# Order of ScalarE's bank copies, and a fifth slot for cached values, in a one-core decoder step

## The chip, the cores and the metric

The kernel runs on one core of one Trainium2 chip. A core has five engines that run their own instruction streams and meet through semaphores: TensorE (matrix products and transposes into the eight PSUM banks), VectorE, ScalarE, GpSimd and SyncE. SyncE (SP in the profile) does nothing here but wait and start DMAs, in the order in which they are written. The metric is the device time of one execution in microseconds. Times inside an execution are counted from the start of the profile's span.

## The reference

One layer of a hybrid decoder, in float32, for two groups of tokens side by side: a prompt of 256 tokens and 8 sample sequences of 4 tokens, together 288 columns.

- `h = RMSNorm(x) @ W_in`, whose columns go to three mixers: a conformer convolution (gated, 31 taps per channel, layer norm, SiLU), an S5 state space with a GELU and a gate (GLU), and a Mamba-2 SSD (4-tap convolution, SiLU, scan over chunks). Their outputs, side by side, are multiplied by `W_out` and added to `x`.
- Cross attention over 256 memory tokens in 4 heads of 512. For the prompt, keys and values are computed: `memn = RMSNorm(mem_prompt)`, `K = memn @ wk`, `V = memn @ wv`. For the samples they are read from caches: 8 batches of K and 8 of V, each 256 x 2048 numbers, that is 2 MB.
- A gated convolution FFN (inner width 5504), and a final RMSNorm.

The outputs are the two groups' results, the new states of all mixers, and the prompt's K and V.

## The kernel before

Activations are kept channels on partitions, tokens along the row: a tile is 128 channels by 288 tokens, and `x` has 16 tiles. A weight matrix is taken in groups of 512 output columns; a group is read in 8 slabs of 512 KB, each two blocks of 128 input rows by 512 columns. Slabs go in turn through the four places of `raw`, and a load is started when the slab four places back has been used.

*Input projection.* Eight groups, `in_group(g)`, over banks 0 to 3, with one output tile of 128 channels in each bank. A slab is 8 products (two passes each, 16 matmul records). Between slabs, `hook_in` places the mixers' work on TensorE by slab number: `glu` products 0 and 1 after slab 50, 2 and 3 after slab 51, exports of states after slabs 56 to 60, the two layer-norm sums of the conformer after 58 and 61. At the first slab of group g TensorE waits, bank by bank, until ScalarE has copied group g-1 out (`in_read`). `in_evac(g)` is that copy. For the sixth group, `in_evac(5)`, it is two `Copy` activations a bank, into `xbr_b`, the input of the 4-tap convolution.

ScalarE's stream is written out by hand. Around the change it reads: squares of the two memory row tiles `mtok` (after their load), then the square root of their mean squares (L1607), then the two scalings of `mtok` (L1610), then `in_evac(5)` (L1569, L1570), then the first tap of each of the 12 convolution tiles (L1587, L1588), then the four gates of S5 (tanh, L1622, and a copy, L1626), each after its `glu` product. The root's input `msum` comes from VectorE, which computes it after the second of the conformer's four channel tiles (L2363; the taps of a tile are the 30 instructions at L2345). After the third tile VectorE does the gating of S5 (`s5_gated`, L2328 and L2321), then the fourth tile, then the 4-tap convolutions (L2373, L2375), and between these the conformer's layer norm (L2386, L2391). `glu` product m uses bank 4 + m % 2, so product 2 waits for the first tanh and product 3 for the second. The memory rows are needed after the eighth group, when TensorE turns them (`turn_mem`).

*Cross attention.* SP starts the cached batches in the order c = 0 to 15 (K 0 to 7, V 0 to 7), each in two halves of 1 MB. `CACHE_SLOT` gives the place of a batch: three slots of `kv`, and as slot 3 the whole of `raw`, free between two weight stages. A load waits until the batch before it in its slot is used: for K by the count of turned tiles, `kc_t` (8 a batch), for V by the count of value batches multiplied, `pv_sample`. TensorE turns the K batches (L1306) and multiplies them with q (L1318), with the prompt's scores, softmax turns and values in between (L731, L1277). Then it does the value batches (`sample_values`, L1328), in the places that `PV_AFTER` gives between the prompt's last heads. All eight value batches are summed in bank 3. ScalarE then copies that bank (`osum`, L1918); the result is turned, and the output projection `xa_wo` begins. On ScalarE the splits of the first two `xa_wo` slabs (L1720; a split makes a high and a low part of the weights) stand ahead of `osum`.

`hhi` and `hlo` (16 tiles each) hold the high and low parts of a projection's input. From the end of the q projection until the prompt's attention results are written there (`o_hi` on ScalarE, `o_lo` on VectorE), they hold nothing.

Of the kernel before, what the change touches and what calls it, by code (L numbers as in the profile page):

```python
# [12 lines left out]
P = 128  # L13
D = 2048
KT = D // P
NP, NB, NL = 256, 8, 4
NS = NB * NL
T = NP + NS
# [15 lines left out]
XH, XD = 4, 512  # L34
NM = 256
MT = NM // P
# [56 lines left out]
def hymba_step(nc, I, O):  # L93
# [3 lines left out]
    def S(name):  # L97
        name = PLACE.get(name, (name, 0))[0]
        if name not in sems:
            sems[name] = ctx.enter_context(nc.semaphore(name))  # L100
        return sems[name]

    def at(name, count):

        return S(name), count + PLACE.get(name, (name, 0))[1]

    def alloc(stack, name, shape, dt=F32):
        return stack.enter_context(nc.sbuf_tensor(name, shape, dt))

    with ctx:  # L110

        def sb(name, shape, dt=F32):
            return alloc(ctx, name, shape, dt)

        ident = sb("ident", [P, P])
# [11 lines left out]
        lev = ExitStack()  # L127
# [8 lines left out]
        lev = ExitStack()  # L136
        raw_lo = alloc(lev, "raw_lo", [P, 4, 1024], F32R)
        lev.close()
        raw = sb("raw", [P, 4, 1024])
# [13 lines left out]
        lev = ExitStack()  # L153
# [6 lines left out]
        lev = ExitStack()  # L160
# [3 lines left out]
        lev = ExitStack()  # L164
        dh2 = alloc(lev, "dh2", [P, 2, 1024], F32R)
        dl2 = alloc(lev, "dl2", [P, 2, 1024], F32R)
        lev.close()
        hhi = sb("hhi", [P, KT, T], F32R)
        hlo = sb("hlo", [P, KT, T], F32R)
        lev = ExitStack()  # L170
        xtok = alloc(lev, "xtok", [P, 3, D])
        lev.close()
        lev = ExitStack()
# [3 lines left out]
        lev = ExitStack()  # L177
# [12 lines left out]
        lev = ExitStack()  # L190
        hT = alloc(lev, "hT", [P, KT, T])
        lev.close()
        lev = ExitStack()
# [15 lines left out]
        lev = ExitStack()  # L209
# [10 lines left out]
        lev = ExitStack()  # L220
# [20 lines left out]
        lev = ExitStack()  # L241
# [20 lines left out]
        lev = ExitStack()  # L262
# [4 lines left out]
        lev = ExitStack()  # L267
# [4 lines left out]
        kv = alloc(lev, "kv", [P, 3, MT, D])  # L272
# [9 lines left out]
        lev = ExitStack()  # L282
# [5 lines left out]
        lev = ExitStack()  # L288
# [11 lines left out]
        lev = ExitStack()  # L300
# [11 lines left out]

        Y_BANK = {(0, 0): 1, (0, 1): 2, (1, 0): 3, (1, 1): 4, (2, 0): 5, (2, 1): 6, (3, 0): 7, (3, 1): 1}

        CACHE_SLOT = [c % 4 for c in range(2 * NB - 1)] + [0]

        def cache(c):

            slot = CACHE_SLOT[c]
            return kv[:, slot, :, :] if slot < 3 \  # L320
                else raw[:, :, :].rearrange("p a b -> p (a b)").rearrange("p (t d) -> p t d", t=MT)

        def cache_loaded(c):

            slot = CACHE_SLOT[c]
            return S(f"kv_loaded{slot}"), 32 * (CACHE_SLOT[:c].count(slot) + 1)

        def turned_p(t):
# [13 lines left out]
        def vsplit(ap, n):  # L342
            return ap.rearrange("p (a b) -> p a b", a=n)
# [33 lines left out]
        PROMPT_AT, PROMPT_STEP = 16, 6  # L377
        KQ = NB * 4
        N_IN_K = 3
        PV_AFTER = {3: (0,), 4: (1, 2), 5: (3,), 6: (4,), 7: (5, 6), 8: (7,)}  # L380

        def prompt_at(q):

# [14 lines left out]
        def slab_dst(slot, width):  # L398
            return raw[:, slot, 0:2 * width].rearrange("p (k n) -> p k n", k=2)
# [28 lines left out]
        def loop(eng, n, body):  # L428

            body(0)  # L430
            with eng.Fori(1, n) as i:
                body(i)
# [8 lines left out]
        def _(sp):  # L441
# [23 lines left out]
            for g, cg_ in enumerate(GORDER):  # L465
                for s in range(8):
# [10 lines left out]
                    if sl in (44, 46):  # L477
                        t = (sl - 44) // 2
# [10 lines left out]
            def split_group(w, g, c0, width=GW, between=None):  # L489
                for s in range(8):  # L490
                    if between:
                        between(s)
                    if isinstance(g, int) and g == G_O and s < 2:
                        continue
                    if isinstance(g, int) and g == 0 and s < 4:
                        wait_used_A(sp, NS_B + s - 4)
                    elif isinstance(g, int) and g == 0 and s < 6:
                        wait_used_B(sp, g, s - 4)
                    else:
                        sp.wait_ge(*at("w_lo", 8 * g + (s - 3)))  # L500
                    sp.dma_start(slab_dst(s % 4, width), slab_src(w, s, c0, width))\
                      .then_inc(S(f"raw_loaded{s % 4}"), 16)

            def four_groups(w, g0):
                loop(sp, 4, lambda i: split_group(w, g0 + i, i * GW))

            k_rows = I["cache_mem_k"][0].rearrange("b (t p) h d -> b p t (h d)", p=P)
            v_rows = I["cache_mem_v"][0].rearrange("b (t p) h d -> b p t (h d)", p=P)
            four_groups(I["w_out"][0], G_OUT)

            def load_cache(c, t):
                sp.dma_start(cache(c)[:, t, :], (k_rows if c < NB else v_rows)[c % NB][:, t, :])\
                  .then_inc(S(f"kv_loaded{CACHE_SLOT[c]}"), 16)


            def early_cache(s):
# [17 lines left out]
            def wo_slabs(slabs):  # L534
                for s in slabs:
                    sp.dma_start(slab_dst(s, GW), slab_src(I["xa_wo"][0], s, 0, GW))\
                      .then_inc(S(f"raw_loaded{s}"), 16)
            for c in range(4, 2 * NB):
                if c == 2 * NB - 1:
                    sp.wait_ge(*at("pv_sample", 4))  # L540
                    wo_slabs((0, 1))
                if c < 12:
                    sp.wait_ge(*at("kc_t", 8 * (c - 3)))
                else:
                    sp.wait_ge(*at("pv_sample", c - 11 if c < 15 else 5))
                for t in range(MT):
                    load_cache(c, t)
            four_groups(I["xa_wo"][0], G_O)

            def gate_up(i):  # L550
# [7 lines left out]
            for half in range(2):  # L558
                c0 = half * DG * P
# [169 lines left out]
        def _(pe):  # L729
# [8 lines left out]
            for n in range(8):  # L738
                t, kb = divmod(n, 4)
# [492 lines left out]
            def never(_):  # L1232
                pass
# [60 lines left out]
            def turn_k(q):  # L1294

                b, d = divmod(q, 4)
                if d == 0:
                    pe.wait_ge(*cache_loaded(b))
                for i in range(2):
                    u = 2 * q + i  # L1300
                    if u >= 3:
                        pe.wait_ge(*at("kc_a", (u - 3) // 2 + 1) if u % 2 else at("kc_v", u // 2 - 1))
                    for hh in range(2):
                        for t in range(MT):
                            c0 = (4 * (2 * i + hh) + d) * P
                            x = pe.transpose(B[5 + u % 3][:, hh * NM + t * P:hh * NM + (t + 1) * P],  # L1306
                                             cache(b)[:, t, c0:c0 + P], ident[:, :])
                    x.then_inc(S("kc_t"), 1)

            def sample_scores(q):  # L1310
# [12 lines left out]
            def sample_values(b):  # L1323

                pe.wait_ge(*cache_loaded(NB + b))
                for t in range(MT):
                    for h in range(XH):
                        x = pe.matmul(B[3][NS * h:NS * (h + 1), 0:XD], lhsT=pTm[:, t, b, NS * h:NS * (h + 1)],  # L1328
                                      rhs=cache(NB + b)[:, t, h * XD:(h + 1) * XD],
                                      start=b == 0 and t == 0, stop=b == NB - 1 and t == MT - 1,  # L1330
                                      tile_position=(0, NS * h))
                x.then_inc(S("pv_sample"), 1)
# [17 lines left out]
            for n in range(N_IN_K, 8 + 1):  # L1350
# [9 lines left out]
                if n < 8:  # L1360
                    p_turn(n)
                for b in PV_AFTER[n]:
                    if b == 0:
# [130 lines left out]
        def _(sc_):  # L1494
            a = sc_.activation
# [59 lines left out]
            def in_evac(g):  # L1555

                for m in range(GM):
                    sc_.wait_ge(*at("in_acc", 4 * g + m + 1))
                    bk = B[m]
                    bs = vsplit(bk[:, NP:T], NB)  # L1560
                    if g == 0:
                        q = a(uT[:, m, :], bk[:, 0:T], ACT.Copy)
                    elif g == 1:
                        q = a(va[:, m, :], bk[:, 0:T], ACT.Copy, scale=0.5)
                    elif g == 2:
                        q = a(th[:, m, :], bk[:, 0:T], ACT.Tanh, scale=0.5)
                    elif g < 6:
                        t = 4 * (g - 3) + m
                        a(xb(t)[:, HC:XP], bk[:, 0:NP], ACT.Copy)  # L1569
                        q = a(xbr_sample(t)[:, :, HC:XS], bs, ACT.Copy)  # L1570
                    else:
                        q = a(zs[:, 4 * (g - 6) + m, :], bk[:, 0:T], ACT.Silu)
                    q.then_inc(S("in_read"), 1)
# [27 lines left out]
            for t in range(MT):  # L1601

                a(zs[:, :, :].rearrange("p a b -> p (a b)")[:, 0:D], mtok[:, t, :], ACT.Square,
                  accum_out=msum[:, t:t + 1]).then_inc(S("mem_sq"), 1)
                sc_.wait_ge(*at("mem_sq", t + 1))
            sc_.wait_ge(*at("mem_v", 1))
            a(msum[:, 2:4], msum[:, 2:4], ACT.Sqrt).then_inc(S("mem_s"), 1)  # L1607
            sc_.wait_ge(*at("mem_v", 2))
            for t in range(MT):
                a(mtok[:, t, :], mtok[:, t, :], ACT.Copy, scale=msum[:, 4 + t:5 + t]).then_inc(S("memn"), 1)  # L1610
            in_evac(5)
            for t in range(12):
                sc_.wait_ge(*at("in_read", 12 + t + 1))
                sc_.wait_ge(*at("s0_turned", XTURNS + 5))
# [1278 lines left out]
```

## Time and profile before

| | us |
|---|---|
| median of 3 runs | 1867.96 (1867.22 to 1871.8) |
| profiled execution | 1866.31 |
| its span, first to last instruction | 1864.6 |
| TensorE busy | 1819.6 (98%) |
| VectorE busy | 1100.0 (59%) |
| ScalarE busy | 704.0 (38%) |
| GpSimd busy | 238.7 (13%) |
| mean granted clock of TensorE | 0.991 |

The profile is of one execution. PE is TensorE's matmul row, PEld its weight loads, DVE is VectorE, ACT ScalarE, POOL GpSimd, SP SyncE. A granted clock of 1.00 is 2.4 GHz and 0.50 is 1.2 GHz. L731 stands for the helper `mm`, through which many products go; operands tell them apart.

### The profile page before, as it was taken

What the parts mean: (1) busy time and instruction counts of PE and PEld (TensorE: products, weight loads), DVE (VectorE), ACT (ScalarE), POOL (GpSimd) and SP (SyncE); (2) the same over time, 40 slices, a digit from 0 to 9 for tenths busy, and PEclk for the clock granted to TensorE, in tenths of its full rate; (3) what the DMA queues carried; (4) which work ended last, traced back from release to release, by engine and by line L of the source; (5) the groups of instructions that cost most, each with busy time, mean ns of one, the idle gap of its engine ahead of it and who ended that gap; (6) DMA issues with size and microseconds to landing.
All of it is one profiled execution on the core that took longest, in us unless ns stands there. A gap on an engine that the chain in (4) does not pass through costs nothing.

```text
span 1864.6 us, 32336 instructions
## 1 busy us (share of the span) xinstructions
PE 1819.6 (98%) x12430; PEld 1646.4 (88%) x12430; DVE 1100.0 (59%) x1926; ACT 704.0 (38%) x1057; POOL 238.7 (13%) x264
## 2 busy tenths in 40 slices
PE   9999979999998999999899999999999999999998
PEld 7877757777666999976799999999999999999998
DVE  6898879655446455443346655655556565446554
ACT  3000242543434343333234444443444445444444
POOL 1024100011214221000032100000000000003300
PEclk9899989999999999999999999999999999999999
DMA  8333523455555657467645555555555545544542
GB/s 247 98 118 112 188 83 123 127 189 181 185 183 174 230 192 270 161 224 268 229 150 167 160 168 161 165 166 160 168 159 167 162 153 167 178 161 158 171 167 97
DMA packets 157955, 316.46 MB, mean 170 GB/s; under 512 B 16938, under 2 KB 39482, under 8 KB 152931
## 3 DMA queue, kind: packets, MB, share of 16 engines
q1 hardware_dynamic: 136098, 295.75, 48.6%
q10 hardware_dynamic: 21771, 19.54, 3.3%
q8 instruction: 57, 0.93, 0.2%
q14 instruction: 29, 0.24, 0.0%
HBM read 300.78 MB, written 14.89 MB: 169 GB/s over the span
## 4 chain that ended last, share of the span: by engine, by line
PE 91%; DVE 4%; ACT 1%; POOL 1%; DMA 1%; issue 1%; ACTq 0%; SPq 0%; POOLq 0%; DVEq 0%
PE bank L731 22%; PE bank L1205 20%; PE bank L1207 20%; PE bank L1206 20%; PE bank L1306 2%; DVE va L2345 2%; PE bank L1318 1%; PE bank L1328 1%; DVE raw_lo L2411 1%; DMA xtok<-in_x_prompt 0%; DMA kv<-in_cache_mem_v 0%; PE bank L800 0%; PE bank L1118 0%; PE bank L940 0%; DVE s L2523 0%
## 5 line engine op out<-in xcount | busy, mean ns | idle before, releaser
L1205 PE MATMUL bank<-hhi,whi 128*128 128x288 f32 x2128 | 631.7, 297 | 1.9 <-DVE hlo L2686 1.5
L1206 PE MATMUL bank<-hlo,whi 128*128 128x288 f32 x2128 | 628.4, 295 | 0.0
L1207 PE MATMUL bank<-hhi,wlo 128*128 128x288 f32 x2128 | 626.4, 294 | 0.0
L2583 DVE TENSOR_TENSOR wlo<-raw,whi 128x1024 fp32r<-128x1024 f32 (+1 forms) x270 | 330.0, 1223 | 375.0 <-ACT whi L1720 374.7
L1720 ACT ACTIVATE whi<-raw 128x1024 fp32r<-128x1024 f32 (+1 forms) x270 | 283.1, 1049 | 507.7 <-PE bank L1207 505.9
L1205 PEld LDWEIGHTS bank<-hhi,whi 128*128 128x128 f32 x2128 | 399.4, 188 | 3.1 <-issue 1.7
L1207 PEld LDWEIGHTS bank<-hhi,wlo 128*128 128x128 f32 x2128 | 401.5, 189 | 0.0
L1206 PEld LDWEIGHTS bank<-hlo,whi 128*128 128x128 f32 x2128 | 400.1, 188 | 0.1
L731 PE MATMUL bank<-hT,raw 128*128 128x288 f32 x1024 | 258.5, 413 | 10.6 <-ACT xbr_b L1570 10.3
L731 PEld LDWEIGHTS bank<-hT,raw 128*128 128x128 f32 x1024 | 195.8, 193 | 67.6 <-issue 14.2
L731 PE MATMUL bank<-khi,mhi 128*128 128x512 f32 x256 | 106.8, 417 | 13.7 <-DVE raw_lo L2411 13.7
L1691 ACT ACTIVATE khi<-raw 128x1024 fp32r<-128x1024 f32 x66 | 69.8, 1058 | 123.4 <-PE bank L731 113.4
L2411 DVE TENSOR_TENSOR raw_lo<-raw,khi 128x1024 fp32r<-128x1024 f32 x66 | 84.8, 1286 | 51.9 <-ACT khi L1691 51.7
L1205 PE MATMUL bank<-ahi,whi 128*128 128x288 f32 x352 | 104.2, 296 | 1.2 <-ACT vtok L1983 1.2
L709 POOL TENSOR_TENSOR cg<-cg,rstd 128x288 f32<-128x288 f32 x43 | 42.8, 994 | 483.1 <-ACT cg L1953 483.1
L1206 PE MATMUL bank<-alo,whi 128*128 128x288 f32 x352 | 104.0, 296 | 0.0
L1207 PE MATMUL bank<-ahi,wlo 128*128 128x288 f32 x352 | 104.0, 295 | 0.0
L731 PE MATMUL bank<-khi,mlo 128*128 128x512 f32 x256 | 101.4, 396 | 0.0
L731 PE MATMUL bank<-raw_lo,mhi 128*128 128x512 f32 x256 | 101.4, 396 | 0.0
L1205 PE MATMUL bank<-ahi,dh 128*128 128x288 f32 x336 | 99.4, 296 | 0.0
L1207 PE MATMUL bank<-ahi,dl 128*128 128x288 f32 x336 | 99.3, 295 | 0.0
L1206 PE MATMUL bank<-alo,dh 128*128 128x288 f32 x336 | 99.2, 295 | 0.0
(507 smaller groups left out, 2346.2 us busy)
## 6 DMA issues: line engine op xcount, KB each, us to landing
raw<-in_ffn_w_down SPq DMA_DIRECT2D x86, 512.0 KB, 3.7
raw<-in_ffn_w_gate SPq DMA_DIRECT2D x80, 512.0 KB, 3.4
raw<-in_ffn_w_up SPq DMA_DIRECT2D x80, 512.0 KB, 3.4
raw<-in_w_in SPq DMA_DIRECT2D x64, 512.0 KB, 3.6
raw<-in_xa_wk SPq DMA_DIRECT2D x32, 512.0 KB, 3.7
raw<-in_xa_wv SPq DMA_DIRECT2D x32, 512.0 KB, 4.1
raw<-in_w_out SPq DMA_DIRECT2D x32, 512.0 KB, 3.6
raw<-in_xa_wq SPq DMA_DIRECT2D x32, 512.0 KB, 3.7
```

Source lines behind the costliest of these rows:

```text
L709: pool.tensor_tensor(cg[:, m, :], cg[:, m, :], rstd[:, :], ALU.mult)\
L731: return pe.matmul(out, lhsT=l, rhs=r, start=start, stop=stop)
L1205: pe.matmul(out, lhsT=wh[:, wo:wo + P], rhs=xh, start=first, stop=False)
L1206: pe.matmul(out, lhsT=wh[:, wo:wo + P], rhs=xl, start=False, stop=False)
L1207: return pe.matmul(out, lhsT=wl[:, wo:wo + P], rhs=xh, start=False, stop=last)
L1306: x = pe.transpose(B[5 + u % 3][:, hh * NM + t * P:hh * NM + (t + 1) * P], cache(b)[:, t, c0:c0 + P], ident[:, :])
L1318: x = pe.matmul(B[3][NS * h:NS * (h + 1), 0:NM], lhsT=qm[:, 4 * h + d, b, :], rhs=kc[:, (2 * q + h // 2) % 4, h % 2, :], start=q == 0, sto ...
L1691: a(khi[:, y % 2, :], raw[:, y % 4, :], ACT.Copy).then_inc(S("kw_hi" if y < NKV else "w_hi"), 1)
L1720: a(whi[:, slot, 0:2 * width], raw[:, s % 4, 0:2 * width], ACT.Copy).then_inc(S("w_hi"), 1)
L2345: q = stt(va[:, t, 0:NP], up[:, t, w:w + NP], wc, va[:, t, 0:NP], ALU.mult, ALU.add)
L2411: tt(raw_lo[:, y % 4, :], raw[:, y % 4, :], khi[:, y % 2, :].bitcast(F32), ALU.subtract)\
L2583: tt(wlo[:, s % 2, wsl], raw[:, s % 4, wsl], whi[:, s % 2, wsl].bitcast(F32), ALU.subtract)\
```

## The change

Two edits. In ScalarE's stream, `in_evac(5)` stands ahead of the wait for the root instead of behind the scalings of the memory rows. And the cached batches get a fifth slot: two pieces of 2048 columns, `vslot_a` in `hhi` (from its tile 8 on) and `vslot_b` in `hlo` (the same). Value batch 0 (c = 8) goes there; its load signals on the semaphore `x_back`, which stood at 16 and comes to 48. The order of loads becomes K 4, 5, V 0, K 6, 7, V 1 to 7, with new places: V 1, 2, 3 in slots 0, 1, 2, V 4 in `raw`, V 5, 6, 7 in slots 0, 1, 2. The first two slabs of `xa_wo` are loaded after the last value batch, and value batches 3 and 4 are multiplied together at step 5.

```diff
+        lev = ExitStack()
+        alloc(lev, "vslot_room_a", [P, 8, T])
+        vslot_a = alloc(lev, "vslot_a", [P, D])
+        alloc(lev, "vslot_room_b", [P, KT * T - D])
+        vslot_b = alloc(lev, "vslot_b", [P, D])
+        lev.close()
         hhi = sb("hhi", [P, KT, T], F32R)
         hlo = sb("hlo", [P, KT, T], F32R)
...
-        CACHE_SLOT = [c % 4 for c in range(2 * NB - 1)] + [0]
-
-        def cache(c):
+        CACHE_SLOT = [0, 1, 2, 3, 0, 1, 2, 3, 4, 0, 1, 2, 3, 0, 1, 2]
+
+        def cache(c, t):
 
             slot = CACHE_SLOT[c]
-            return kv[:, slot, :, :] if slot < 3 \
-                else raw[:, :, :].rearrange("p a b -> p (a b)").rearrange("p (t d) -> p t d", t=MT)
+            if slot == 4:
+                return (vslot_a, vslot_b)[t][:, :]
+            return kv[:, slot, t, :] if slot < 3 \
+                else raw[:, :, :].rearrange("p a b -> p (a b)")[:, t * D:(t + 1) * D]
 
         def cache_loaded(c):
 
             slot = CACHE_SLOT[c]
+            if slot == 4:
+                return S("x_back"), 48
...
-        PV_AFTER = {3: (0,), 4: (1, 2), 5: (3,), 6: (4,), 7: (5, 6), 8: (7,)}
+        PV_AFTER = {3: (0,), 4: (1, 2), 5: (3, 4), 6: (5,), 7: (6,), 8: (7,)}
...
-            for c in range(4, 2 * NB):
-                if c == 2 * NB - 1:
-                    sp.wait_ge(*at("pv_sample", 4))
-                    wo_slabs((0, 1))
-                if c < 12:
+            for c in (4, 5, 8, 6, 7, 9, 10, 11, 12, 13, 14, 15):
+                if c < 8:
                     sp.wait_ge(*at("kc_t", 8 * (c - 3)))
+                elif c == 8:
+                    sp.wait_ge(*at("q_read", 16))
+                elif c < 13:
+                    sp.wait_ge(*at("kc_t", 8 * (c - 4)))
                 else:
-                    sp.wait_ge(*at("pv_sample", c - 11 if c < 15 else 5))
+                    sp.wait_ge(*at("pv_sample", c - 11))
                 for t in range(MT):
                     load_cache(c, t)
+            sp.wait_ge(*at("pv_sample", 5))
+            wo_slabs((0, 1))
             four_groups(I["xa_wo"][0], G_O)
...
                 sc_.wait_ge(*at("mem_sq", t + 1))
+            in_evac(5)
             sc_.wait_ge(*at("mem_v", 1))
             a(msum[:, 2:4], msum[:, 2:4], ACT.Sqrt).then_inc(S("mem_s"), 1)
             sc_.wait_ge(*at("mem_v", 2))
             for t in range(MT):
                 a(mtok[:, t, :], mtok[:, t, :], ACT.Copy, scale=msum[:, 4 + t:5 + t]).then_inc(S("memn"), 1)
-            in_evac(5)
```

The remaining lines of the diff only pass the half t to `cache` and name the semaphore of the load.

## Rows read from the trace of the kernel before

**Rows 1.** Waits of TensorE: source, us in total, times, longest.
```profile
PE bank L731 <- ACT xbr_b L1570: 10.3, 1, 10.3
...
PE bank L1328 <- DMA kv<-in_cache_mem_v: 3.4, 1, 3.4
```

**Rows 2.** Timeline of TensorE, 235 to 330: start, us, instructions [idle before].
```profile
252.65 13.50 PE L731 MATMUL bank<-hT,raw 128*128 128x288 f32 x48 [10.35 <-ACT xbr_b L1570]
...
277.62 19.56 PE L731 MATMUL bank<-hT,raw 128*128 128x288 f32 x80
```

**Rows 3.** Timeline of ScalarE, 225 to 330.
```profile
246.51 1.28 ACT L1607 ACT_TABLE_LOAD   x1 [13.47 <-DVE msum L2363]
247.81 0.20 ACT L1607 ACTIVATE msum<-msum 128x2 f32<-128x2 f32 x1
...
252.04 0.36 ACT L1569 ACTIVATE xbr_b<-bank 128x256 f32<-128x256 f32 x1
...
253.41 0.66 ACT L1587 ACTIVATE xc<-xbr_a,prm 128x256 f32<-128x256 f32 x1
...
263.14 1.28 ACT L1622 ACT_TABLE_LOAD   x1
268.13 0.50 ACT L1622 ACTIVATE hbuf<-bank,gcol_b 128x288 f32<-128x288 f32 x1 [3.71 <-PE bank L731]
```

**Rows 4.** Stretches: us, engines' busy us (instructions), clock, DMA share, GB/s.
```profile
250.00:252.60 2.60, 0.00 (x0) 0.00 (x0) 2.46 (x6) 2.60 (x5) 0.00 (x0) 0.50 0.00 0
...
252.60:256.20 3.60, 3.55 (x8) 2.67 (x9) 3.42 (x6) 3.60 (x13) 0.00 (x0) 0.54 0.00 0
...
470.20:474.20 4.00, 1.96 (x9) 1.62 (x10) 2.44 (x2) 2.78 (x5) 3.96 (x5) 1.00 1.08 341
...
333.90:340.90 7.00, 4.02 (x12) 3.20 (x12) 6.10 (x12) 5.98 (x15) 0.00 (x0) 0.78 0.17 58
```

**Rows 5.** Timeline of SP's DMA starts, value batches 5 and 7.
```profile
879.41 0.80 SPq L512 DMA_DIRECT2D kv<-in_cache_mem_v  x2
...
892.69 0.82 SPq L512 DMA_DIRECT2D kv<-in_cache_mem_v  x2
```

**Rows 6.** Timeline of TensorE, 800 to 930.
```profile
845.88 1.09 PE L1306 MATMUL bank<-ident,kv 128*128 128x128 f32 x8
...
884.92 1.92 PE L1328 MATMUL bank<-raw,pTm 128*32 128x512 f32 x16
...
901.76 3.24 PE L1328 MATMUL bank<-kv,pTm 128*32 128x512 f32 x16 [3.36 <-DMA kv<-in_cache_mem_v]
```

**Rows 7.** Timeline of VectorE, 246 to 362.
```profile
263.58 3.09 DVE L2345 SCALAR_TENSOR_TENSOR va<-up,prm,va 128x256 f32<-128x256 f32 x6
...
279.70 4.12 DVE L2345 SCALAR_TENSOR_TENSOR va<-up,prm,va 128x256 f32<-128x256 f32 x8
...
324.52 0.46 DVE L2391 TENSOR_SCALAR rstd<-bank 128x288 f32<-128x288 f32 x1 [1.70 <-PE bank L731]
```

**Rows 8.** Waits of VectorE, 260 to 285.
```profile
DVE hbuf L2328 <- ACT hbuf L1622: 9.6, 4, 5.0
```

**Rows 9.** Stretches of the cached batches' loads, columns as above.
```profile
814.00:846.00 32.00, 32.00 (x323) 20.32 (x322) 14.63 (x24) 13.96 (x24) 0.00 (x0) 1.00 0.87 327
874.00:902.00 28.00, 24.64 (x195) 15.13 (x198) 8.53 (x20) 7.08 (x16) 0.00 (x0) 0.98 0.96 362
882.00:900.00 18.00, 16.40 (x131) 10.01 (x129) 6.44 (x13) 5.64 (x12) 0.00 (x0) 1.00 1.00 396
880.00:882.00 2.00, 2.00 (x17) 1.03 (x10) 0.34 (x1) 0.00 (x0) 0.00 (x0) 1.00 0.90 221
```

**Rows 10.** DMA issues: source, engine, count, KB each, median us to landing.
```profile
raw<-in_ffn_w_up SPq DMA_DIRECT2D x80, 512.0 KB, 3.4
```

**Rows 11.** Timeline of ScalarE, 892 to 908.
```profile
895.40 2.00 ACT L1720 ACTIVATE whi<-raw 128x1024 fp32r<-128x1024 f32 x2
905.08 0.60 ACT L1918 ACTIVATE osum<-bank 128x512 f32<-128x512 f32 x1 [7.67 <-PE bank L1328]
```

More of the change, by code:

```diff
@@ L511, in load_cache @@
             def load_cache(c, t):
-                sp.dma_start(cache(c)[:, t, :], (k_rows if c < NB else v_rows)[c % NB][:, t, :])\
-                  .then_inc(S(f"kv_loaded{CACHE_SLOT[c]}"), 16)
+                sp.dma_start(cache(c, t), (k_rows if c < NB else v_rows)[c % NB][:, t, :])\
+                  .then_inc(S(f"kv_loaded{CACHE_SLOT[c]}" if CACHE_SLOT[c] < 4 else "x_back"), 16)
             def early_cache(s):
@@ L1306, in turn_k @@
                             x = pe.transpose(B[5 + u % 3][:, hh * NM + t * P:hh * NM + (t + 1) * P],
-                                             cache(b)[:, t, c0:c0 + P], ident[:, :])
+                                             cache(b, t)[:, c0:c0 + P], ident[:, :])
                     x.then_inc(S("kc_t"), 1)
@@ L1328, in sample_values @@
                         x = pe.matmul(B[3][NS * h:NS * (h + 1), 0:XD], lhsT=pTm[:, t, b, NS * h:NS * (h + 1)],
-                                      rhs=cache(NB + b)[:, t, h * XD:(h + 1) * XD],
+                                      rhs=cache(NB + b, t)[:, h * XD:(h + 1) * XD],
                                       start=b == 0 and t == 0, stop=b == NB - 1 and t == MT - 1,
```

## The prediction
> **What bounds the kernel now.** I read the busy table and the chain of waits first: TensorE is busy 98% of the span and carries most of the chain. What an edit to other engines can win is therefore TensorE's idle time, and the waits by engine list it [rows 1]: one wait of 10.3 us on ScalarE's bank copies and one of 3.4 us on the last half of a value batch are its two longest. The change touches both. Around each I read the engines in order of time.
>
> *First pause.* TensorE ends the sixth input group at 242.3 and resumes at 252.65 [rows 2]. ScalarE finished its squares at 233.0 and then sat 13.47 us before the `Sqrt`, which waits for VectorE's `msum`; the two scalings of the memory rows follow, and only then the copies that free the banks, from 252.04 [rows 3]. VectorE is busy with the 31 taps all that time. The pause is paid twice: the granted clock is 0.54 for the next 3.6 us [rows 4], mostly its 1.2 GHz level. The next 48 matmuls take 13.50 us, where 80 at full clock take 19.56 [rows 2], 11.7 for 48: 1.8 us more.
>
> *Second pause.* Value batch 7 is issued when batch 4 is used up, at 892.69 [rows 5]; TensorE is ready at 898.4 and goes on at 901.76. The clock has fallen by then: this batch's 16 matmuls take 3.24 us where batch 3's took 1.92 [rows 6].
>
> **Part 1: the copies ahead of the root.** Eight `Copy` activations move; they issue no DMA. They wait for the group's four accumulators, which end about 1 us apart up to 242.3 (a slab of 16 matmuls takes 3.9, a quarter of it for each tile), and ScalarE is free then, so the last copy is done by 242.9. TensorE enters the next group with bank 0, free since about 240: no pause. Queued behind the copies on ScalarE is the `Sqrt`, whose input comes at 246.4 anyway; it and the scalings keep their times.
>
> What is late next is the gating of S5. TensorE does three slabs (11.7) to 254.0, two GLU products (3.9) to 257.9 and one slab to 261.8; its third GLU product needs the bank that the first tanh reads. ScalarE's 24 first taps start at 252.04 instead of 253.41, so they end 1.37 earlier, at 261.77, the table load (1.28) at 263.05 and the tanh (0.50) at 263.55 [rows 3]. TensorE stands 1.8 us. A pause of 2 us left the clock at 1.00 [rows 4], so I charge no clock. The third and fourth product end at 267.4, where they ended at 277.62 [rows 2]: TensorE is 10.2 us earlier from here.
>
> VectorE decides how much of that stays. Its third channel tile ends at 266.67 in both versions [rows 7]. The gating behind it took 13.03 us, of which 9.6 were waits for late tanhs [rows 8]. With the first two tanhs there, 3.4 us of work remain and about 1.3 of waits (two tanhs of 0.5, short copies), say 4.75: its fourth tile starts at 271.4 instead of 279.70, 8.3 earlier. From there it had no gap until a wait of 1.70 us for the second layer-norm sum [rows 7]. That gives a cap of 8.3 + 1.7 = 10.0; TensorE's sum is 10.2 earlier, and ScalarE's squares, queued behind its export DMAs, move with TensorE. I take 9.9. What follows (layer norm, Silu, memory split, first K product) hangs on that one value. TensorE's 3 us pause before the first K product stays, and its clock loss. Later waits of the mixers are relative to it.
>
> Ends: 10.0, the cap; 8.5, if the gating costs another round of 0.9 and 0.5 is lost elsewhere.
>
> *A rule against this part.* The table load before the root takes 1.28 us and its activation starts 0.02 after it [rows 3]. The Trainium skill, page "ScalarE: Activation LUTs", section "What ACT_TABLE_LOAD costs", gives a switch to another set about 2.66 us, 1.38 of them a drain. By it the first tanh would come at 264.9, TensorE would stand 3.2 us and part 1 would give 8.6. The row shows no drain.
>
> **Part 2: a fifth cache slot.** Value batch 0 goes to columns of `hhi` and `hlo` (tiles 8 to 15), loaded behind K batch 5 instead of behind K batch 7; batches 1 to 3 move to slots 0 to 2 and wait for a K batch that is one earlier; batch 4 takes `raw` when K batch 7 is turned, where it waited for value batch 0 to be used. Batches 5 and 6 keep their issue times (879.41 [rows 5] and some 2 us later), batch 7 goes from the end of batch 4 to the end of batch 3, and the first two slabs of `xa_wo` move behind it on SP, past its two 1 MB loads.
>
> *What is delayed.* Batch 0's two loads stand ahead of K batch 6 on SP. The new wait there, on the last q read, is met before TensorE turns its first K tile, so the loads queued behind it lose nothing by it. The bytes do cost: K batches 4 and 5, value batch 0 and K batch 6, four times 2.1 MB from 814 at 327 GB/s [rows 9], land near 839.7; TensorE wants K batch 6 at 845.88 [rows 6]. Six us of cover: cost nothing. Without it each us would be one on the path.
>
> *What is gained.* TensorE's order becomes batches 0; 1, 2; 3, 4; 5; 6; 7, the same work, so without a wait batch 7 starts at 898.4. Batch 3 ends 1.9 us after 884.92 [rows 6]: batch 7 is issued near 887. Of a load's landing time, 3.4 us for 512 KB [rows 10], bytes at 396 GB/s [rows 9] explain 1.3, so I estimate 2.1 as fixed. Batches 5, 6, 7 then land at 879.41 + 2.1 + 15.9 (6.29 MB) = 897.4, before 898.4. The values end at 900.3 instead of 905.0: 3.36 of wait and 1.3 of clock, 4.7 us.
>
> *What takes it back.* On ScalarE the two `xa_wo` splits (2.00 us the pair) stand ahead of the `osum` copy (905.08 to 905.68) [rows 11]. Their data was there at 895.4; now 1.05 MB follow batch 7 and land 2.65 later, at 900.0. The second split ends at 901.05, `osum` at 901.65; TensorE has 1 us of other products there, to 901.3. About 0.5 late: part 2 gives 4.2. Ends: 4.7 without delay; with the mean of 874 to 902, 362 GB/s [rows 9], slabs at 901.8 and a gain of 2.4; at the 221 GB/s of the worst 2 us [rows 9], a loss (D below).
>
> *A rule here.* The Trainium skill, page "DMA: Bandwidth & Descriptors", section "Bandwidth", holds the HBM side to about 358 GB/s per core. By it batch 7 would land at 899.1, the slabs at 902.0, and part 2 would give 2.2. The 396 GB/s over 18 us decide.
>
> **Sum.** 9.9 + 4.2 = 14.1 us. The profiled execution took 1866.31 us, its span being 1864.6; it becomes 1852.2. The median shown, 1867.96, lies 1.65 above it, so the forecast for a median is 1853.8, 0.76% faster.
>
> **Rivals.**
> *A. Batch 7 or the `xa_wo` slabs come late and part 2 gives next to nothing.* For it: the engines are 0.96 busy from 874 to 902 [rows 9], and the slabs lose their lead. Against: 2.1 MB leave that stretch for the K phase. Time: 1867.96 − 9.9 = 1858.
> *B. The third GLU product is held long enough for the clock to fall again.* For it: after a pause of 3 us the clock was low (mean 0.78 over pause and the 4 us after it [rows 4]). Against: the 2 us pause. Price: 1.8 us of slow matmuls as after the first pause, up to 3 with the longer pause itself; part 1 gives 7 to 8.1, time 1855.5 to 1857. The drain that the Trainium skill states (above) would bring such a pause about.
> *C. The 10.3 us pause had another cause that ends as late,* such as the group's weights. Against: the DMA engines were idle from 250 on [rows 4], so the weights had landed. Part 2 alone: 1864.
> *D. Slower: the backlog of value batches holds the output projection.* Place: `osum`, behind the `xa_wo` splits. At 221 GB/s the 7.34 MB land at 914.7 and `osum` ends at 916.4, 10.7 later than before, which eats part 1: 1869. Below that rate the kernel is slower than before: 1874 at 190 GB/s. For it: one window of 2 us; against: 18 us around it.
>
> **How the numbers follow.** Forecast 0.68, own range 1851 to 1856.5; A 0.13, B 0.10, C 0.06, D 0.03. 0.3% is 5.6 us, about what a measurement of this kernel tells from no change: below 1862.4 is faster. Forecast, A and B are: 0.91. C lies within: 0.06. D is slower: 0.03. The range takes in A and B: 1850.5 to 1859.5; its lower end is the sum at its best (14.7) less 2.8 us, the runs shown having spread over 4.6.
>
> **What would show it.** Right: no idle of TensorE on the sixth group's copies, granted clock 1.00 through the seventh group, a new wait of about 1.8 us before the third GLU product, the second layer-norm sum read near 314.6, the first K product near 327; then no wait for the last value batch and an `osum` held by ScalarE's own splits for under a microsecond. Wrong: VectorE's fourth tile later than 273 (part 1 is smaller), a pause over 2.5 us at the third GLU product, any idle before K batch 6 or a value batch, or the `xa_wo` splits later than 902.

## Result and profile after

The changed kernel takes 1849.35 us (median of 4 runs, 1848.13 to 1851.55) against 1867.59 (4 runs, 1866.77 to 1871.8) for the one before, run beside it: ratio 0.9903, 95% interval 0.9891 to 0.9915, 18.2 us by the medians. The forecast was 1853.8 with a range from 1850.5. The sign, the end of both pauses and the new waits came as forecast; the gain is 4.45 us larger, and the time lies 1.15 us below the range. The profiled execution took 1848.65 us (span 1846.9, mean granted clock 0.995), 17.66 less than the one before.

The first view to read is again TensorE's list of waits (source, us in total, times, longest).

```profile
PE bank L744 <- DVE raw_lo L2424: 14.4, 10, 3.0
...
PE bank L744 <- ACT hbuf L1635: 0.6, 1, 0.6
...
PE bank L1383 <- ACT osum L1931: 0.3, 1, 0.3
```

Both waits of [rows 1] are gone. In their places stand the two that the prediction named, before the third GLU product (0.6, forecast 1.8) and on `osum` (0.3, forecast about 0.5). The longest that is left, 3.0 us before the first K product, was there before.

**The first pause.** TensorE in order of time (start, us, instructions, idle before and its releaser), to be laid beside [rows 2]:

```profile
224.74 29.02 PE L744 MATMUL bank<-hT,raw 128*128 128x288 f32 x119
253.59 4.04 PE L744 MATMUL bank<-uT,glu_w 128*128 128x288 f32 x16
257.47 4.04 PE L744 MATMUL bank<-hT,raw 128*128 128x288 f32 x16
262.12 4.15 PE L744 MATMUL bank<-uT,glu_w 128*128 128x288 f32 x16 [0.60 <-ACT hbuf L1635]
266.11 19.56 PE L744 MATMUL bank<-hT,raw 128*128 128x288 f32 x80
```

The first line runs through the place where 10.35 us of idle stood. The 80 matmuls that started at 277.62 start at 266.11: 11.5 us earlier, where 10.2 were forecast. The clock there, in the window view with the columns of [rows 4] (the second row is for part 2, below):

```profile
250.00:256.00 6.00, 6.00 (x26) 4.71 (x25) 5.71 (x10) 6.00 (x15) 0.00 (x0) 1.00 0.49 129
...
869.00:887.00 18.00, 18.00 (x146) 11.30 (x146) 4.07 (x11) 3.94 (x11) 0.00 (x0) 1.00 0.99 397
```

ScalarE shows where the extra came from; the lines answer to [rows 3]:

```profile
242.15 0.39 ACT L1582 ACTIVATE xbr_b<-bank 128x256 f32<-128x256 f32 x1 [0.49 <-PE bank L744]
...
242.65 1.28 ACT L1621 ACT_TABLE_LOAD   x1
246.34 0.20 ACT L1621 ACTIVATE msum<-msum 128x2 f32<-128x2 f32 x1 [2.41 <-DVE msum L2376]
246.78 3.90 ACT L1624 ACTIVATE mtok<-mtok,msum 128x2048 f32<-128x2048 f32 x2 [0.23 <-DVE msum L2378]
250.58 0.59 ACT L1600 ACTIVATE xc<-xbr_a,prm 128x256 f32<-128x256 f32 x1
...
260.27 1.28 ACT L1635 ACT_TABLE_LOAD   x1
261.57 0.89 ACT L1635 ACTIVATE hbuf<-bank,gcol_b 128x288 f32<-128x288 f32 x2
```

The root's table load stands at 242.65, right behind the copies, and waits for nothing; the root alone waits. Before, the load started at 246.51, behind VectorE's mean squares, and the root 1.30 after it. So the root comes 1.47 earlier, and with it the scalings, the first taps and the tanh, which starts at 261.57 (forecast 263.05). VectorE answers to [rows 7]:

```profile
246.58 0.17 DVE L2378 RECIPROCAL msum<-msum 128x2 f32<-128x2 f32 x1 [0.27 <-ACT msum L1621]
...
262.14 3.09 DVE L2358 SCALAR_TENSOR_TENSOR va<-up,prm,va 128x256 f32<-128x256 f32 x6
...
269.99 4.12 DVE L2358 SCALAR_TENSOR_TENSOR va<-up,prm,va 128x256 f32<-128x256 f32 x8
```

Its own wait for the root, 1.61 us before, is 0.27, so its third tile ends at 265.23 and not at 266.67. The gating behind it takes 4.76 us to the fourth tile, where 4.75 was forecast. The second layer-norm sum is read at 313.02 (forecast 314.6), the first K product starts at 325.38 (forecast about 327).

**The second pause.** TensorE at the end of the values, beside [rows 6]:

```profile
859.79 1.06 PE L1341 MATMUL bank<-vslot_a,pTm 128*32 128x512 f32 x8 [0.34 <-ACT pTm L1924]
...
884.62 3.64 PE L1341 MATMUL bank<-kv,pTm 128*32 128x512 f32 x32
888.19 1.16 PE L744 MATMUL bank<-pT,vtok 128*128 128x128 f32 x8
889.69 0.66 PE L1383 MATMUL bank<-ident,osum 128*128 128x128 f32 x4 [0.34 <-ACT osum L1931]
...
892.74 0.37 PE L1218 MATMUL bank<-hhi,whi 128*128 128x288 f32 x1 [1.50 <-DVE hlo L2699]
```

The last batch is one block of 32 matmuls in 3.64 us, without the wait and without the slow half. ScalarE's `xa_wo` splits, beside [rows 11]:

```profile
888.09 1.06 ACT L1733 ACTIVATE whi<-raw 128x1024 fp32r<-128x1024 f32 x1 [0.23 <-DMA raw<-in_xa_wo]
889.05 0.58 ACT L1931 ACTIVATE osum<-bank 128x512 f32<-128x512 f32 x1
```

The second split is the last thing that a transfer holds, for 0.23 us, and `osum` stands right behind it. The engines moved 397 GB/s over 18 us here (second row of the windows above); the estimate used 396. The Trainium skill, page "DMA: Bandwidth & Descriptors", section "Bandwidth", puts the HBM side at about 358 per core for transfers from HBM, and in the same section calls that the share of each core when both cores of a pair stream. Only one core works here, and this window lies above it.

### The profile page after: what moved, and what is told of

Same layout as the page of the kernel before. It is cut to its first block, busy times and chain, and to the rows that moved or that the text cites. A ratio compares the mean times of both kernels' runs of the same rounds, so it can differ in the third digit from the quotient of the medians.

```text
span 1846.9 us, 32336 instructions
## 1 busy us (share of the span) xinstructions
PE 1815.1 (98%) x12430; PEld 1643.9 (89%) x12430; DVE 1099.5 (60%) x1926; ACT 704.5 (38%) x1057; POOL 239.4 (13%) x264
## 4 chain that ended last, share of the span: by engine, by line
PE 88%; DVE 8%; ACT 2%; DMA 1%; issue 1%; POOL 0%; ACTq 0%; SPq 0%; DVEq 0%; POOLq 0%
PE bank L1218 21%; PE bank L1220 20%; PE bank L1219 20%; PE bank L744 19%; DVE va L2358 3%; PE bank L1319 2%; PE bank L1331 1%; DVE xc L2386 1%; DVE raw_lo L2424 1%; DMA raw<-in_xa_wo 1%; DMA xtok<-in_x_prompt 0%; PE bank L1341 0%; DVE s L2536 0%; PE bank L813 0%; PE bank L953 0%
```

## Where the time went, by stage

Each stage is measured between two instructions of the same trace, so that differences earlier in the execution drop out. "Mean squares" is VectorE's `msum` (L2363; L2376 in the changed kernel), "K turns" is the first score product behind the cached phase's start, "last turns" the final transposes. In us:

| | mean squares to first K product | to K turns | to output projection | to last turns |
|---|---|---|---|---|
| before | 90.62 | 467.71 | 104.32 | 941.63 |
| after | 79.24 | 467.37 | 99.99 | 940.10 |
| less | 11.38 | 0.34 | 4.33 | 1.53 |
| forecast | 9.9 | 0 | 4.2 | 0 |

With 0.13 from the start these make 17.7. Part 2 is sized right, part 1 is 1.5 short, and 1.5 fell in a stage that the change doesn't touch.

## Experiments

**One part alone.** E1 is the kernel before with the copies moved:

```
             for t in range(MT):
                 ...
                 sc_.wait_ge(*at("mem_sq", t + 1))
+            in_evac(5)
             sc_.wait_ge(*at("mem_v", 1))
             ...
-            in_evac(5)
```

> The copies ahead of the root, without the fifth slot. Theory L (the table load): by moving the copies, the root's table load of 1.28 us comes out from behind its wait, so VectorE too is 1.5 us earlier. Then this edit alone brings the first K product from 336.89 to about 325.4 and the kernel gains 11.5 to 12.5 us (about 1855.5). Rival S (the sum as forecast, 9.9, the rest of the difference being the level of TensorE's clock in single executions): the first K product near 327 and a gain of 9.9, with any more seen as clock. In both the 3.4 us wait on the last value batch stays.

It took 1855.15 us (5 runs) against 1867.45 (20 runs): 0.9933 [0.9919, 0.9946]. Its load stands ahead of the wait too:

```profile
240.47 1.28 ACT L1608 ACT_TABLE_LOAD   x1
244.15 0.20 ACT L1608 ACTIVATE msum<-msum 128x2 f32<-128x2 f32 x1 [2.40 <-DVE msum L2363]
```

Mean squares to first K product is 79.22 us, the pause at the third GLU product 0.60: as in the full change. So the 11.4 us of the first stage are part 1's alone. Its wait for the last value batch is still there (3.69 us).

E2 is the other part, the cache slot of the diff, with `in_evac(5)` where it was.

> The fifth cache slot, without the copies' move. Both theories: first pause of 10.3 us stays, values end 4.7 to 4.9 us earlier counted from the first K turn, osum held by the output projection's splits by about 0.5 us, gain 4.2 us (about 1863.3). If the two parts do not add up (copies only + slot only against both together, 18.2), something couples them; theory L expects them to add up within 1.5 us.

It took 1863.42 us (10 runs): 0.9977 [0.9967, 0.9986]. TensorE's pause on the copies is 10.4 us, the wait for the last value batch is gone, and from K turns to the output projection it takes 100.03 us, 4.29 less than before. E2 keeps the slot, the new order of loads and the later `xa_wo` slabs together; what each of them gives was not tried apart. ScalarE's load is behind the wait again:

```profile
246.30 1.28 ACT L1620 ACT_TABLE_LOAD   x1 [13.50 <-DVE msum L2376]
```

The medians give 12.3 and 4.0, together 16.3, against 18.2 for both. That is 1.9 apart, where at most 1.5 was expected; the intervals, some 2 us either way on each, do not tell it from nothing.

**The table load.** What decides where it stands? The trace also records the instructions that only wait, which the timelines leave out. ScalarE's around the root, by start in us, with the semaphore that each waits for (`act_setup` carries the counts of `mem_sq`); before, then after:

```
246.47 L1606 EVENT_SEMAPHORE [waits mem_v]
246.51 L1607 ACT_TABLE_LOAD
247.81 L1607 ACTIVATE msum<-msum 128x2 [waits act_setup]

242.65 L1621 ACT_TABLE_LOAD
246.34 L1621 ACTIVATE msum<-msum 128x2 [waits mem_v]
```

In the code before, two waits stand in a row ahead of the root, `mem_sq` 2 and `mem_v` 1. The root carries the first; the second is an instruction of its own, and the load stands behind that. In the code after, the first copy carries the `mem_sq` wait, the root carries `mem_v`, and no wait stands ahead of the load. E3 puts a second wait back, which is long met, into the changed kernel:

```
             in_evac(5)
+            sc_.wait_ge(*at("mem_sq", 2))
             sc_.wait_ge(*at("mem_v", 1))
```

> The kernel after, with one wait added that is long met: a second wait, on mem_sq, right before the root's wait on mem_v. Theory L: a load in front of an instruction with two waits takes one of them; it takes mem_v, as before, so the load stands at about 246.4 again instead of 242.65. Then the memory scalings start about 248.2 instead of 246.8, TensorE's wait at the third GLU product is 1.8 to 2.1 us instead of 0.6, VectorE's fourth tile starts about 271.4 instead of 269.99, the first K product comes at 326.8 instead of 325.38, and the kernel loses 1.4 us against the kernel after (1850.8). Rival S: nothing moves, since a met wait costs nothing.

It took 1851.83 us (5 runs): 0.9922 [0.9908, 0.9936] of before. The theory as written above puts the wait on the load; by the trace it is again an instruction of its own ahead of the load (at 245.95, L1621), and the root carries `mem_sq`. ScalarE and TensorE of E3, and its clock:

```profile
246.00 1.28 ACT L1622 ACT_TABLE_LOAD   x1 [3.70 <-DVE msum L2377]
247.29 0.20 ACT L1622 ACTIVATE msum<-msum 128x2 f32<-128x2 f32 x1
```

```profile
263.08 5.84 PE L744 MATMUL bank<-uT,glu_w 128*128 128x288 f32 x16 [1.90 <-ACT hbuf L1636]
```

```profile
260.00:264.00 4.00, 2.10 (x9) 1.34 (x9) 3.75 (x9) 3.39 (x7) 0.00 (x0) 1.00 0.39 116
264.00:268.00 4.00, 4.00 (x11) 2.87 (x10) 3.21 (x8) 0.85 (x3) 0.00 (x0) 0.57 0.04 15
```

E3 is the kernel that the prediction had in mind, its time lies inside the stated range, and it behaves so: VectorE waits 1.61 us for the root, TensorE stands 1.90 (forecast 1.8), and VectorE's fourth tile starts 25.17 us after the mean squares (forecast 271.4 − 246.27 = 25.13; after: 23.85). What the forecast ruled out came as well: the clock falls behind that pause, and 16 matmuls take 5.84 us for 4.15. Mean squares to first K product is 82.25 us, 3.0 more than after. So the load's place is worth 3.0 us in this trace, some 1.7 of it clock (4 us at 0.57), and 2.0 to 2.5 by the medians (1849.35 and 1849.81 for the changed kernel). The intervals of E3 and of the changed kernel overlap, so the size rests on the traces.

E4 does the opposite: the kernel before, without the second of the two waits (the `mem_v` wait, which VectorE raises after both squares, covers it).

```
-                sc_.wait_ge(*at("mem_sq", t + 1))
+                if t == 0:
+                    sc_.wait_ge(*at("mem_sq", 1))
```

> The kernel before, without ScalarE's second wait on mem_sq (VectorE waits for the same count before it gives the root its input, so the order stays). Theory L: the table load runs at 233 in ScalarE's idle time, the root and all behind it come 1.5 us earlier, TensorE's pause before the seventh group is 8.9 us instead of 10.35, VectorE's wait at L2365 is 0.3 instead of 1.6, the kernel gains 1.4 to 1.5 us (about 1866.1). Rival S: no change beyond 0.3 us.

It took 1865.15 us (11 runs): 0.9984 [0.9975, 0.9993], 1.3 to 4.7 us faster by one wait that holds nothing. ScalarE and TensorE of E4:

```profile
233.22 1.28 ACT L1608 ACT_TABLE_LOAD   x1
246.63 0.20 ACT L1608 ACTIVATE msum<-msum 128x2 f32<-128x2 f32 x1 [12.12 <-DVE msum L2364]
247.06 3.90 ACT L1611 ACTIVATE mtok<-mtok,msum 128x2048 f32<-128x2048 f32 x2 [0.23 <-DVE msum L2366]
```

```profile
251.46 13.97 PE L731 MATMUL bank<-hT,raw 128*128 128x288 f32 x48 [9.04 <-ACT xbr_b L1570]
```

The load runs at 233.22, behind the squares, and the root carries the `mem_v` wait. VectorE's wait for the root is 0.27 instead of 1.61 and TensorE's pause 9.04 instead of 10.35 (forecast 0.3 and 8.9). E3 and E4 together settle it: a wait that is met long before costs a load's length when it makes the other wait an instruction of its own ahead of the load.

**The same kernels again.** E5 is the changed kernel once more, E8 the one before, run together with E6 and E7.

> The kernel after, unchanged, a second time. What the table load does not explain of the miss (18.2 measured, 9.9 + 1.5 + 4.2 = 15.6 worked out) should be the places where TensorE's clock falls by chance: 1.7 us each, at the pause before the first K product, at the pauses of the K and V projection, and behind the small transposes before the FFN. Theory L with chance: the same first K product (325.4 from the same start), but low stretches at other places than in the first profile, and a median between 1848 and 1852. If the low stretches are the change's own doing, they stand at the same places and the median is 1849.4 within 1 us.

> The kernel before, unchanged, a second time. The pause of 10.3 us and the wait on the last value batch (3.4 us within 1 us) come again; of the low stretches of the clock, those behind these two come again, and those at the first K product and behind the small transposes may or may not.

E5: 1849.81 us (4 runs, 1848.07 to 1851.59) against 1868.29 (7 runs): 0.9901 [0.9885, 0.9918]. From mean squares to the first K product it takes 79.26 us, as in the first trace. The last stage of E5 takes 941.61 us, like that of the kernel before (941.63) and not like that of the same kernel's first trace (940.10). The windows say why: E5's clock, then the first trace's, in the same columns.

```profile
914.00:916.00 2.00, 2.00 (x11) 2.00 (x10) 0.00 (x0) 0.00 (x0) 0.00 (x0) 0.52 0.77 227
916.00:918.00 2.00, 2.00 (x12) 2.00 (x12) 0.00 (x0) 0.03 (x1) 0.00 (x0) 0.63 0.00 0
```

```profile
572.00:574.00 2.00, 1.40 (x4) 1.12 (x5) 1.69 (x2) 0.83 (x1) 1.92 (x2) 0.68 0.83 231
574.00:576.00 2.00, 2.00 (x6) 1.63 (x5) 0.29 (x1) 0.00 (x0) 1.84 (x3) 0.50 0.91 279
...
912.00:915.00 3.00, 3.00 (x23) 3.00 (x24) 0.47 (x2) 0.00 (x0) 0.00 (x0) 1.00 0.51 175
```

One kernel, two executions, and the clock falls in different places, each time for some 3 us. In the last stage the fall costs 1.5 us. Over all ten profiles of the two kernels and their variants this stage takes 941.6 in five and 940.0 to 940.1 in five, whatever the edit was. E5's profiled execution took 1851.14 us; against that of before it gains 15.2 and not 17.7.

E8 took 1868.08 us in its one run, mean clock 0.991. The pause on the copies and the wait for the last value batch (4.4 us) came again. Behind its pause before the first K product the clock stays at 1.00, and its last stage takes 940.10, so each of the two kernels has shown both times there. Two more things differ. Behind the pause on the copies the clock stays low for longer, and a pause of 2.05 us is followed by a low clock, where the pause of 2.04 us from 470.20 ([rows 4]) was not:

```profile
251.40 14.84 PE L731 MATMUL bank<-hT,raw 128*128 128x288 f32 x48 [10.34 <-ACT xbr_b L1570]
...
471.67 0.50 PE L731 MATMUL bank<-khi,mhi 128*128 128x512 f32 x1 [2.05 <-DVE raw_lo L2411]
```

```profile
472.00:476.00 4.00, 4.00 (x12) 3.05 (x10) 2.24 (x1) 0.41 (x1) 1.60 (x1) 0.57 0.71 231
```

The 48 matmuls take 14.84 us where the first trace has 13.50, and mean squares to first K product takes 91.95 where it has 90.62. E2, with the copies where they were, has 14.72 and 91.84. So the 11.4 us of part 1 belong to one execution of the kernel before; against these two it gains 12.6 to 12.7, near E1's 12.3 by medians.

**Two tries for more.** E6 moves 8 of the 12 SiLUs that stand ahead of the first K product to before the last state export, where ScalarE waits anyway (`conv_silu(t)` is the wait and the SiLU of tile t).

```
             for r in range(5):
+                if r == 4:
+                    for t in range(8):
+                        conv_silu(t)
...
-            for t in range(12):
+            for t in range(8, 12):
```

> The kernel after, with the first 8 of the 12 SiLUs of the 4-tap convolution moved on ScalarE from behind the layer-norm root to ahead of the last state export, where ScalarE waits 2.6 us. If the chain root, SiLUs, splits on ScalarE holds the first K product, as read from the profile after (313.5 to 325.4), that product comes 2.7 us earlier, TensorE's pause before it is 0.3 instead of 2.98 us, its clock never falls there, and the kernel gains 2.7 to 3.5 us against the kernel after. If VectorE's layer norm holds it (reciprocal 1.95 and four scalings 1.8 behind the root), the gain is under 1 us.

It took 1849.49 us (4 runs): 0.9904 [0.9887, 0.992], the same as E5. The moved SiLUs are 2.7 us of ScalarE, but the pause before the first K product shrinks by 1.1 only, between what the two theories gave. TensorE and ScalarE of E6:

```profile
319.30 1.91 PE L990 MATMUL bank<-ident,mtok 128*128 128x128 f32 x16
323.09 0.50 PE L744 MATMUL bank<-khi,mhi 128*128 128x512 f32 x1 [1.89 <-DVE raw_lo L2430]
```

```profile
319.99 0.84 ACT L1703 ACTIVATE mhi<-bank,prm 128x256 fp32r<-128x256 f32 x2 [1.45 <-PE bank L990]
```

ScalarE is now early and waits for TensorE's own transposes of the memory rows; what follows them (its split, then VectorE's) is the rest of the pause.

E7 is E6 with the `osum` copy ahead of the second `xa_wo` split.

```
             split(G_O, 0)
-            split(G_O, 1)
             sc_.wait_ge(*at("pv_sample", NB))
             a(osum[:, :], B[3][:, :], ACT.Copy).then_inc(S("osum"), 1)
+            split(G_O, 1)
```

> The kernel of the early SiLUs, and on ScalarE the copy of the summed values (osum) ahead of the second split of the output projection's weights. If that split holds osum in the kernel after (0.34 us of TensorE's idle, osum at 889.05 for values that end at 888.2), that idle goes and the second split still comes before the weights are wanted: 0.3 to 0.6 us less than the early SiLUs alone, not resolved in the median, read in the profile.

It took 1850.51 us (4 runs, 1846.97 to 1851.85): 0.991 [0.9893, 0.9926]. The wait on `osum` (0.5 us in E6, 0.3 in the changed kernel) is gone, and the next one is 0.3 longer (1.5 in E6):

```profile
PE bank L1218 <- DVE hlo L2705: 1.8, 1, 1.8
```

From K turns to the output projection E7 takes 99.73 us, against 100.17 in E6 and 99.99 in the changed kernel: 0.4 and 0.3 less, in one profile each. By their medians neither is told apart from the changed kernel, so no better version came of them.

## Why the prediction was off

*Right.* Part 1's pause is gone and the clock holds 1.00 through the seventh group. The new waits came at both places. Part 2's estimates hold: last batch without a wait, values ending 4.89 earlier against K turns (forecast 4.7), the turns of `osum` 0.5 later behind them (forecast about 0.5), together 4.33 for 4.2. No batch of the K phase came late. Rival C falls with the first TensorE timeline, A and D with the second.

*The step that failed* is "Queued behind the copies on ScalarE is the `Sqrt`, whose input comes at 246.4 anyway; it and the scalings keep their times", and with it "Its third channel tile ends at 266.67 in both versions". What is queued there first is the root's table load. That it started behind the wait in the trace of before was taken as fixed. It hung on the two waits in a row, of which one stood ahead of the load and which the moved copies separate (E3, E4). So the root, its scalings and the third tile do not keep their times: they come 1.4 to 1.5 us earlier. The rows had a hint: the tanh's load, at 263.14 in [rows 3], had run ahead of the tanh's own wait of 3.71 us, so a load need not wait for what its activation waits for, and the one at 246.51 called for a reason.

*Its size.* The gain to VectorE's fourth tile is 33.43 − 23.85 = 9.58 where the step had 8.3. The 1.3 more is the fall of VectorE's wait for the root (1.61 to 0.27). From there to the first K product another 1.80 was gained (forecast 1.7, less 0.1 for the sum's slack). Hence 11.4 for 9.9, against the trace that the forecast was read from.

*A second error was covered by the first.* "so I charge no clock" did not hold for the pause that was forecast: in E3's profile a pause of 1.90 us lowered the clock to 0.57 over 4 us. That was rival B, at a tenth. The row that the step leaned on, a pause of 2 us at a clock of 1.00, did not come again in E8, where the same kernel has a pause of 2.05 us and then 0.57. So the term was open, and the sum put it at nothing. By E3's profile part 1 without the early load would have given 90.62 − 82.25 = 8.4 us. With it the pause is 0.6 and the clock stays; that this hid the term was luck.

*The rest of the miss.* The profiled execution misses by 17.66 − 14.1 = 3.6 us: 1.5 of part 1, 1.5 from the last stage, and under 0.4 each from the others. The last stage's part is not the change's: E5 takes the longer time there and E8 the shorter. The other 0.9 of the 4.45 is the step from profiled execution to median: 1.65 were added, and the runs after lie 0.70 above theirs. The longer low clock behind the first pause, as in E8 and E2, would make part of that step; this is not shown. With the load's 1.5 us in the sum the forecast would have been 1852.3 and the range's lower end 1849.0, with the measured 1849.35 inside it, if only just.

*The page on table loads.* The Trainium skill, page "ScalarE: Activation LUTs", section "What ACT_TABLE_LOAD costs", counts a drain of about 1.38 us with each switch. By the row at 260.27 the tanh starts 0.02 us after the load ends, as the root did in [rows 3], and the last first tap ends 0.02 us ahead of the load: no drain shows.

## What to carry to other kernels

When a block moves ahead of a waiting activation that needs a table load, ask where each wait stands, before and after: where the activation alone carried it, the load ran in idle time; where a wait stood ahead of the load as an instruction of its own, the load was on the path with its 1.28 us (E3, E4). A wait that is always met can be worth taking out for that reason alone (E4). And where TensorE's pauses are 2 to 3 us, read two executions before a difference of 1.5 us is put down to an edit.

## What the runs showed of the hardware

- A pause of nearly the same length leaves TensorE's clock at 1.00 in one execution and lowers it in another. Before the first K product the pause is 3.0 us in E1 and in the changed kernel; the granted clock from 322 to 330 is 0.79 in the first and 1.00 in the second. Of the eight profiles with this pause four have a low clock behind it (before, E1, E3, E4):

```profile
322.00:330.00 8.00, 6.82 (x25) 5.53 (x26) 5.59 (x10) 5.89 (x14) 0.00 (x0) 0.79 0.15 46
```

```profile
322.00:330.00 8.00, 4.20 (x21) 3.13 (x20) 6.95 (x14) 7.47 (x19) 0.00 (x0) 1.00 0.22 69
```

- The clock also fell where TensorE had been 2.00 of 2.00 us busy, a microsecond after 43 transposes of 16x16 (E5, 914 to 918), which the first trace of the same kernel passed at 1.00. The pauses of 9 to 10.4 us and of 3.4 to 4.4 lowered it each time; 0.6 us did not. In between it went both ways: 1.90 us in E3 and 2.05 in E8, E2 and E5 lowered it, 2.04 in the first trace of before and 1.89 in E6 (1.00 from 322 to 332) did not. What decides there stays open; it wasn't tried.
